# First weight split, norm-weight wait and last outputs in the last stage of a hybrid decoder step

## What is computed

```python
    ya = (y * jax.nn.silu(g_r)) @ w_proj_a
    yb = (u * s * jax.nn.silu(g_g)) @ w_proj_b
    m = jax.nn.sigmoid(gate_a) * ya + jax.nn.sigmoid(gate_b) * yb
    return h + m @ w_out, new_shift, S, vn
...
def rms_norm(x, g):
    xf = x.astype(jnp.float32)
    y = xf * lax.rsqrt(jnp.mean(xf * xf, axis=-1, keepdims=True) + RMS_EPS)
    return (y * g).astype(x.dtype)
...
    y_prompt = rms_norm(hp, final_norm_g)
```

## Time and profile before

| | us |
|---|---|
| median of 3 runs | 3621.11 |
| lowest, highest | 3619.23, 3623.88 |
| profiled execution, in all | 3622.61 |
| its span | 3620.9 |
| PE busy in the span | 3439.6 |
| DVE, ACT, POOL busy | 1756.8, 1152.7, 883.1 |

### The profile page before, as it was taken

How to read it: one execution, slowest core, us unless ns; L and a number is a source line. 1 busy time by engine, 2 the same in 40 slices (tenths; PEclk the granted TensorE clock), 3 DMA queues, 4 the chain that set the end, 5 groups by cost and what they waited for, 6 DMA issues and landing times. The chain is left out here.

```text
span 3620.9 us, 60687 instructions
## 1 busy us (share of the span) xinstructions
PE 3439.6 (95%) x25742; PEld 3329.3 (92%) x25742; DVE 1756.8 (49%) x2100; ACT 1152.7 (32%) x1325; POOL 883.1 (24%) x1494
## 2 busy tenths in 40 slices
PE   8999999996999999899999899999786799999998
PEld 7999999996999999899999899999774799999997
DVE  6333233223555555555555655555236455554653
ACT  2000000002444444544444444443224333433432
POOL 0000000001444444344434344444014003103112
PEclk9999999998999999999999999999798899999999
DMA  4111111114545545554545454554344555555564
GB/s 165 72 70 60 68 72 72 61 50 157 156 137 147 148 136 156 143 144 140 147 138 149 145 151 138 148 147 140 99 134 159 187 175 171 179 194 177 184 209 137
DMA packets 338449, 494.35 MB, mean 137 GB/s; under 512 B 219762, under 2 KB 282754, under 8 KB 306308
## 3 DMA queue, kind: packets, MB, share of 16 engines
q1 hardware_dynamic: 325364, 460.64, 41.1%
q10 hardware_dynamic: 12240, 28.77, 2.1%
q0 software_dynamic: 576, 1.08, 0.1%
HBM read 412.49 MB, written 77.90 MB: 135 GB/s over the span
## 5 line engine op out<-in xcount | busy, mean ns | idle before, releaser
L511 PE MATMUL st_acc<-st_xh,st_wh 128*128 128x364 f32 (+1 forms) x2688 | 914.9, 340 | 36.8 <-DVE st_wl L471 27.5
L511 PE MATMUL st_acc<-st_xh,st_wl 128*128 128x364 f32 (+1 forms) x2688 | 888.9, 331 | 0.0
L511 PE MATMUL st_acc<-st_xl,st_wh 128*128 128x364 f32 (+1 forms) x2688 | 887.8, 330 | 0.0
L511 PEld LDWEIGHTS st_acc<-st_xh,st_wh 128*128 128x128 f32 x2688 | 511.8, 190 | 46.5 <-issue 22.7
L471 DVE TENSOR_TENSOR st_wl<-st_raw,st_wh 128x2048 fp32r<-128x2048 f32 x168 | 395.8, 2356 | 259.9 <-ACT st_wh L441 259.8
L511 PEld LDWEIGHTS st_acc<-st_xh,st_wl 128*128 128x128 f32 x2688 | 511.1, 190 | 2.0
L511 PEld LDWEIGHTS st_acc<-st_xl,st_wh 128*128 128x128 f32 x2688 | 510.5, 190 | 0.0
L441 ACT ACTIVATE st_wh<-st_raw 128x2048 fp32r<-128x2048 f32 x168 | 321.5, 1914 | 420.4 <-PE st_acc L511 418.0
L175 PE MATMUL fr_acc<-fr_xh,fr_wh 128*128 128x364 f32 x1584 | 355.1, 332 | 1.5 <-issue 1.5
L175 PE MATMUL fr_acc<-fr_xl,fr_wh 128*128 128x364 f32 x1584 | 349.4, 329 | 0.0
L175 PE MATMUL fr_acc<-fr_xh,fr_wl 128*128 128x364 f32 x1584 | 349.1, 328 | 0.0
(11 more groups left out here) (213 smaller groups left out, 5212.2 us busy)
## 6 DMA issues: line engine op xcount, KB each, us to landing
st_raw<-in_w_in SPq DMA_DIRECT2D x168, 1024.0 KB, 5.3
tl_raw<-in_w_proj SPq DMA_DIRECT2D x48, 1024.0 KB, 5.1
tl_raw<-in_w_out SPq DMA_DIRECT2D x48, 1024.0 KB, 4.9
fr_raw<-in_w_in SPq DMA_DIRECT2D x33, 1024.0 KB, 4.8
z<-st_stage SPq DMA_DIRECT2D x168, 182.0 KB, 5.5
z<-fr_stage ACTq DMA_DIRECT2D x33, 548.0 KB, 2.7
tl_gate<-z SPq DMA_DIRECT2D x64, 192.0 KB, 2.5
zrk<-z SPq DMA_DIRECT2D x68, 128.0 KB, 5.6
```

The source lines that it names most:

```text
L511: mm = pe.matmul(self.acc[s][:, w], wt[s][:, k * P:(k + 1) * P], x[:, k, w], start=(k == 0 and wt is self.wh and x is self.xh), stop=(k == ...
```

## The change

Three things change in `phase_tail`.

1. DVE awaits the norm weights no longer ahead of its first operand tile but behind the 16 tiles, ahead of the first merge.
2. The split of unit 0's weights stands behind operand tile 0 instead of tile 3, on ACT (`high(0)`) and on DVE (`low(0)`).
3. Of the last piece's 16 outputs, those with n = 3, 7, 11 and 15 are POOL's. Each is two instructions there: `tl_h` times the column of norm weights, in place, and then times `tl_rs` into `tl_o[3]`, with a wait on a new semaphore in between. Ahead of both POOL waits for the reciprocal, the norm weights and the store of the buffer's last use. SP's stores keep their order of n; that of an output of POOL waits for a second new semaphore.

```diff
+        self.hg_ready, self.o3_ready = sem("tl_hg_ready"), sem("tl_o3_ready")
...
                 def store(q, n):
-                    sp.wait_ge(tl.o_ready, done(q, n))
+                    if q == NP - 1:
+                        sp.wait_ge(*((tl.o3_ready, n // 4 + 1) if n % 4 == 3 else (tl.o_ready, q * KT + n - n // 4 + 1)))
+                    else:
+                        sp.wait_ge(tl.o_ready, done(q, n))
...
+                def output(q, n):
+                    w = slice(0, width(q))
+                    pool.wait_ge(tl.rs_ready, q + 1)
+                    pool.wait_ge(tl.g_loaded, 16)
+                    pool.wait_ge(tl.stored[n % 4], (q * KT + n) // 4 * 16)
+                    pool.tensor_scalar(tl.h[:, n, w], tl.h[:, n, w], tl.g_sb[:, n:n + 1], None, MUL).then_inc(tl.hg_ready, 1)
+                    pool.wait_ge(tl.hg_ready, n // 4 + 1)
+                    pool.tensor_tensor(tl.o[n % 4][:, w], tl.h[:, n, w], tl.rs[:, w], MUL).then_inc(tl.o3_ready, 1)
...
+                for n in range(3, KT, 4):
+                    output(NP - 1, n)
...
                     x_high(0, n)
                     if n + 4 < KT:
                         feed(0, n + 4)
-                    if n == 3:
+                    if n == 0:
                         high(0)
...
-                dve.wait_ge(tl.g_loaded, 16)
                 for n in range(KT):
                     x_low(0, n)
-                    if n == 3:
+                    if n == 0:
                         low(0)
                     if n == KT - 4:
                         low(1)
+                dve.wait_ge(tl.g_loaded, 16)
...
                 scale(NP - 1)
                 for n in range(KT):
-                    output(NP - 1, n)
+                    if n % 4 != 3:
+                        output(NP - 1, n)
```

## The result

The changed kernel takes 3627.45 us (median of 20 runs, 3623.76 to 3631.55), the kernel before beside it 3621.49 (20 runs, 3619.23 to 3625.44). The ratio is 1.0014, 95% interval 1.0008 to 1.0021: slower by 0.14%, which is 5 to 6 us. The forecast was 3626.6.

A forecast was written before the change was run, and what follows sets the result against it. PE, busy for 95% of the span, was taken as the bound, with the ring of four output buffers limiting the end. Start -1.1 and end +6.6 gave +5.5 us on the median 3621.1: 3626.6, range 3621.5 to 3629.5.

The forecast's parts named there:

- POOL's loop: End of the stage: 4.26 us a round, store to landing 1.80, then S, one DVE output, T; +4.8 us.
- The wait for the norm weights: Start of the stage: with it moved, DVE starts operand tile 0 at about 2813.59 instead of 2814.70, gain 1.1 us.
- The step on the clock: Behind PE's pause: half speed for 3.5 us taken as unchanged, at nothing; a full-speed restart would give -1.6 more.
- The split: Start of the stage: PE's first matmul at about 2818.8 instead of 2824.56, which doesn't reach the chain of waits.
- S: POOL's first instruction for each of its outputs, h times the norm weights: taken as 1.0 us, bounds 0.46 and 1.06.
- T: POOL's second instruction for each of its outputs, times the reciprocal: 0.86 us, one DVE output of 0.46 after S.
- The first round: End of the stage, outputs 0 to 3: store 3 at 3611.4 instead of about 3609.6, +1.8 us.
- The slow first landing: End of the stage: first store landing halfway between 1.8 and 2.5 us, +0.35; 0.7 in the highest case, +8.5.
- GpSimd cheaper than its rows: Rival at the end: no lock, or S near 0.46; rounds of 3.3 to 3.9 us, say 3623; chance 0.20.
- Its share hidden: Rival at the end: POOL's outputs ready when SP stores them, not slower; -1.6 in all, 3619.5; chance 0.05.
- A dearer lock: Rival at the end: two DVE outputs between S and T, or slower S; up to +7.4, 3628.5; chance 0.21.
- Weights late: Rival at the start: first weights land later than 2814.5, 1.1 us lost, 3627.7; chance counted within the forecast's 0.54.

The follow-up runs named there:

- The 1280 columns: The kernel before plus a GpSimd tensor_scalar and tensor_tensor of 128x1280, results unread, beside the last outputs: end 17.8 us behind the reciprocal instead of 13.3.

## Why the prediction was right, and where its steps were off

**Time and sign** held: 3627.45 in a range of 3621.5 to 3629.5, +6.0 on the medians and +4.7 on the marks of the trace, for a forecast of +5.5. The mechanism that was named, POOL's loop through the buffer and its landing, is what the chain shows, and shortening the loop shortened the end. Measured apart, the loss at the end shows in median and trace, the gain at the start in traces alone. That the total came within 1 us of the forecast is in part luck: the steps below were off by up to 1.3 us, in both directions, and the runs of the changed kernel spread over 8.

**The wait for the norm weights**: right at its place, 1.1 us at DVE's first tile (5.45 instead of 6.55). PE's restart gained 1.26, because the operand load that was to lose 0.3 lost 0.17 (DVE's tiles behind it start at 2819.65 and 2821.34, 1.69 apart where the pace is 1.52). The step on the clock failed. I took the slow restart as unchanged, and wrote that a full-speed restart would be worth 1.6. The price was right for the stretch that it was read from (766.1 against 764.45), but the stretch isn't unchanged: of the 1.26 us that the restart came earlier 0.33 was lost in a longer stretch at half clock. Its length went from 3.7 to 5.9 us over the traces, and PE loses about half of it.

**The split**: nothing by itself, as forecast and as the kernel with the split alone shows. The weights' cover held: ACT's copy at 2810.94 waited for DVE's tile and the load's issue, not for the weights.

**POOL's loop**: the sum is nearly right, 4.08 to 4.17 a round for 4.26, but from terms that were off both ways.
- S was 1.09, not 1.0: a little above the upper end, the row taken by columns. A part that doesn't grow does exist. The 1280 columns took 3.88, less the 0.36 for which the first S of the changed kernel waited in the same place (1.45 against 1.09), so 3.52; against 1.09 for 320 that is 2.54 ns a column, and an estimated 0.27 us that doesn't grow. The row of 256 columns multiplied by a constant, and S by a column; whether that is the rest wasn't tried.
- From landing to the start of S it took 0.19, not DVE's 0.09: 3610.61 + 1.81 = 3612.42, and S at 3612.61.
- No DVE output came between S and T (forecast 0.46): T started 0.07 behind S. The turn-taking of the earlier trace rows was carried over whole, and a short tensor_scalar lets DVE in some 0.76 us ahead of its own end, so DVE's output ran within S and was through or nearly so.

**The first round** is the term that failed most. I had T behind output 1 and output 2 behind T, +1.8. DVE got outputs 1 and 2 in while S was still recorded as running:

```profile
3603.55 0.82 DVE L1902 SCALAR_TENSOR_TENSOR tl_o<-tl_h,tl_g,tl_rs 128x320 f32<-128x320 f32 x1
...
3604.29 0.54 DVE L1902 SCALAR_TENSOR_TENSOR tl_o<-tl_h,tl_g,tl_rs 128x320 f32<-128x320 f32 x1
```

The first was held 0.27, the second not at all. Store 3 left at 3605.57, 2.5 us behind the first output; it was 2.0 before and 3.8 in the forecast. So +0.5, and 1.3 of the forecast's excess lies here. The slow first landing took a part back: 2.76 us, 0.96 above a later one, where I had added 0.35 and the upper bound 0.7.

**Rivals.** GpSimd cheaper than its rows: no, S lay at the upper end. Its share hidden: no, even with the ring gone it loses 1.55. A dearer lock: the upper bound wasn't reached, because DVE's outputs did their waiting behind T and not the reverse; in two rounds one of them was held there for 0.6,

```profile
3609.78 1.14 DVE L1902 SCALAR_TENSOR_TENSOR tl_o<-tl_h,tl_g,tl_rs 128x320 f32<-128x320 f32 x1
```

which costs nothing, since its store has to wait for POOL's anyway. Weights late: no. The lock itself is as the Trainium skill ("SBUF — State Buffer", section "SBUF: two separate sides") has it in that both engines' instructions exclude each other, also a scalar_tensor_tensor and a tensor_scalar; "for the whole instruction" the traces don't bear out, with 0.64 and 0.19 us let go at the end of the long instructions, by their recorded ends.

## What to carry to other kernels

Ask what a round waits for before sharing its work: here four buffers waited for their stores to land, DVE had a fifth of each round free, and a slower engine with one of these buffers made every round as long as its own turn. Taking the ring away (the outputs in place, 2.3 us off the end) was worth more than the helper that was tried, which lost time with the ring and without it. A gain ahead of a PE that restarts at half clock may come out smaller than it went in: look at PEclk behind the pause, and at what PE could do in it.

## What the runs showed of the hardware

- A GpSimd tensor_scalar (fp32, by a column) of 128x320 takes 1.07 to 1.09 us, longer than a two-input tensor_tensor of the same shape, 0.86 to 0.88.
- GpSimd and DVE exclude each other for scalar_tensor_tensor against tensor_scalar too: an output of 0.54 took 3.38 beside 1280 columns. Taking its last 0.54 as the undisturbed output, it was let in 0.64 us ahead of the recorded end of the tensor_scalar, and 0.19 ahead of that of a tensor_tensor.
- The moment at which PE's clock rose behind the same pause moved from 3.7 to 5.9 us behind the restart between the traces, and with it the time up to the last reciprocal by up to 1.0 us; matmuls with unread results ahead of the pause held it at full speed.
- Stores of 160 KB landed in 1.8 to 2.0 us, but for some early ones of the ring: stores 0 to 3 of the kernel before took 2.5 to 2.7, and in the changed kernel stores 0 to 2 took 1.8 and stores 3 to 6 2.2 to 2.8. With the outputs in place none of the sixteen was slow. Why, wasn't tried.
